# Four transposes of an expert step taken apart and put among the next step's first weight matmuls

## The reference, cut to what matters

```
h = silu(xb @ w_gate[e]) * (xb @ w_up[e])     # 128 rows x inner width
y = h @ w_down[e]                             # 128 rows x 1024
```

## Time and profile before

| | |
|---|---|
| median of 3 runs | 2444.83 us (2444.14 to 2445.98) |
| profiled execution, first to last instruction | 2444.1 us |
| PE busy | 2319.3 us, 95% of the span |
| DVE busy | 1842.5 us, 75% |
| ACT busy | 1472.0 us, 60% |
| instructions | 30601 |
| mean granted TensorE clock | 0.975 |

### The profile page before, as it was taken

The page is one execution under the profiler, slowest core; times in us unless marked ns, Lnnn a source line. Parts: engine busy times, 40 slices in busy tenths (PEclk is TensorE's granted clock), DMA queues, the critical chain, the costliest instruction groups (busy, mean ns, idle before and its releaser), DMA issues.

```text
span 2444.1 us, 30601 instructions
## 1 busy us (share of the span) xinstructions
PE 2319.3 (95%) x12418; PEld 1890.2 (77%) x12418; DVE 1842.5 (75%) x1911; ACT 1472.0 (60%) x1441; POOL 39.0 (2%) x41
## 2 busy tenths in 40 slices
PE   7989989999999998988999998899999999999996
PEld 6778777888888886776788777678888888888885
DVE  5885558888898985676454577588988878888885
ACT  5355437776777774535443653476776767767764
POOL 0100000000000000020000002000000000000000
PEclk8999998999999999999999999899999999999999
DMA  9444446999999996506455451269999989999991
GB/s 233 127 122 143 143 161 218 363 367 359 366 358 366 356 369 213 162 8 192 157 188 181 160 162 53 82 222 363 356 363 361 356 300 346 361 365 357 366 345 40
DMA packets 281225, 617.62 MB, mean 253 GB/s; under 512 B 31848, under 2 KB 130408, under 8 KB 243696
## 3 DMA queue, kind: packets, MB, share of 16 engines
q1 hardware_dynamic: 279664, 611.33, 71.9%
q10 hardware_dynamic: 1408, 4.19, 0.5%
HBM read 612.34 MB, written 1.05 MB: 251 GB/s over the span
## 4 chain that ended last, share of the span: by engine, by line
PE 83%; DVE 10%; ACT 4%; issue 2%; DMA 0%; DVEq 0%; ACTq 0%; SPq 0%
PE ps L566 24%; PE ps L567 24%; PE ps L568 24%; DVE ring_parts L590 3%; ACT high_parts L586 2%; PE ps L2153 1%; PE ps L2809 1%; PE ps L2123 1%; PE ps L3090 1%; PE ps L2124 1%; PE ps L3103 1%; DVE arena L1357 0%; DVE arena L3347 0%; PE ps L1559 0%; PE ps L2164 0%
## 5 line engine op out<-in xcount | busy, mean ns | idle before, releaser
L590 DVE TENSOR_TENSOR ring_parts<-ring,high_parts 128x2048 fp32r<-128x2048 f32 (+1 forms) x574 | 1283.0, 2274 | 172.8 <-ACT high_parts L586 166.8
L586 ACT CAST high_parts<-ring 128x2048 fp32r<-128x2048 f32 (+1 forms) x574 | 1078.7, 1898 | 185.1 <-PE ps L568 181.6
L568 PE MATMUL ps<-high_parts,arena_parts 128*128 128x512 f32 (+2 forms) x1560 | 619.8, 397 | 0.0
L566 PE MATMUL ps<-high_parts,hT_parts 128*128 128x512 f32 (+2 forms) x1120 | 456.9, 408 | 30.4 <-DVE ring_parts L590 12.1
L567 PE MATMUL ps<-ring_parts,hT_parts 128*128 128x512 f32 (+2 forms) x1120 | 445.5, 398 | 0.0
L566 PE MATMUL ps<-high_parts 128*128 128x512 f32 x912 | 365.3, 401 | 0.0
L567 PE MATMUL ps<-ring_parts,high_parts 128*128 128x512 f32 x912 | 359.1, 394 | 0.0
L568 PE MATMUL ps<-high_parts 128*128 128x512 f32 x912 | 356.5, 391 | 0.0
L568 PEld LDWEIGHTS ps<-high_parts,arena_parts 128*128 128x128 f32 x1560 | 299.1, 192 | 68.8
L566 PE MATMUL ps<-high_parts,arena_parts 128*128 128x512 f32 x744 | 293.6, 395 | 5.3 <-DVE arena_parts L1869 2.9
L567 PE MATMUL ps<-ring_parts,arena_parts 128*128 128x512 f32 x744 | 292.7, 393 | 0.0
(11 more groups left out here) (531 smaller groups left out, 1828.0 us busy)
## 6 DMA issues: line engine op xcount, KB each, us to landing
ring<-in_moe_w SPq DMA_DIRECT2D x248, 1024.0 KB, 5.4
ring<-in_w_gate SPq DMA_DIRECT2D x64, 1024.0 KB, 5.3
ring<-in_w_up SPq DMA_DIRECT2D x64, 1024.0 KB, 5.3
ring<-in_w_down SPq DMA_DIRECT2D x64, 1024.0 KB, 5.3
ring<-in_w_in SPq DMA_DIRECT2D x104, 256.0 KB, 4.4
ring<-in_ffn_w SPq DMA_DIRECT2D x44, 512.0 KB, 4.8
ring<-in_w_in SPq DMA_DIRECT2D x20, 1024.0 KB, 5.1
ring<-in_moe_w SPq DMA_DIRECT2D x32, 512.0 KB, 4.9
```

What stands on the lines that cost most here:

```text
L566: pe.matmul(dst, a_hi, b_hi, start=first, stop=False, skip_group_check=True)
L568: return pe.matmul(dst, a_lo, b_hi, start=False, stop=last, skip_group_check=True)
L586: act.copy(high_flat(p), raw_flat(p)).then_inc(upper, 1)
L590: dve.tensor_tensor(raw_flat(p, ring_parts_flat), raw_flat(p), f32(high_flat(p)), ALU.subtract).then_inc(split, 1)
```

## The change

The four transposes of a turn no longer stand together ahead of the next step's first gate piece. A new function `turn_chunk` makes one transpose; `up(st, 0, between)` calls it after each of its four chunks, so that one transpose follows every third matmul. The two waits of `turn` go with the first of the transposes. When the held step is a short one, only the first two chunks are followed by one. At the two kinds of places where a turn is not in front of a plain step (`grouped` steps, the second step of each block, the end of each block) it stays as it was: 75 turns of 80 are moved, 288 transposes of 304. The signal `used` of the piece is still given by its twelfth matmul, in front of the last transpose. The number of instructions that compute something is the same.

```diff
+            def turn_chunk(st, c):
+                nc_ = st.n // P
+                if c == 0:
+                    pe.wait_ge(sig("moe_hid"), st.no)
+                    if st.no > 1:
+                        pe.wait_ge(sig("moe_hidT"), st.no - 1)
+                mm = pe.transpose(ps[:, TURN, c * P:(c + 1) * P], m_hid[:, 0:st.n][:, c::nc_], ident[:])
+                if c == nc_ - 1:
+                    mm.then_inc(sig("moe_turned"), 1)
+
             def turn(st):
-                pe.wait_ge(sig("moe_hid"), st.no)
-                if st.no > 1:
-                    pe.wait_ge(sig("moe_hidT"), st.no - 1)
-                nc_ = st.n // P
-                for c in range(nc_):
-                    mm = pe.transpose(ps[:, TURN, c * P:(c + 1) * P], m_hid[:, 0:st.n][:, c::nc_], ident[:])
-                mm.then_inc(sig("moe_turned"), 1)
+                for c in range(st.n // P):
+                    turn_chunk(st, c)
...
-            def up(st, h):
+            def up(st, h, turned=None):
...
                     mm = matmul3(pe, ps[:, bank, :], hi[:, c, :], lo[:, c, :], a[:, i], b[:, i], c == 0, c == KC - 1)
-                mm.then_inc(used, 1)
+                    if i == 3:
+                        mm.then_inc(used, 1)
+                    if turned and i < turned.n // P:
+                        turn_chunk(turned, i)
...
-                if held and s > 1:
+                grouped = st.first and b % TOGETHER == 0
+                between = held if s > 1 and not grouped else None
+                if s > 1 and grouped:
                     turn(held)
-                grouped = st.first and b % TOGETHER == 0
...
-                up(st, 0)
+                up(st, 0, between)
```

## The result

The changed kernel takes 2466.12 us (median of 6 runs, 2461.41 to 2469.07), the kernel before 2444.48 us (median of 6, 2440.91 to 2448.57). The ratio is 1.0088, 95% interval 1.0076 to 1.0100: slower by 0.9%. Forecast were 2468.4 us in a range of 2460 to 2481. The profiled execution took 2469.07 us; its span is 2467.3 us, 23.2 us over that of the profiled execution of before.

The account below looks back on a forecast made before the run. PE was taken to bound the kernel, busy 95% of the span. Plain steps 0, short steps 18.8 and filled waits 4.8 us gave 23.6 us more: 2468.4 us, range 2460 to 2481.

Parts of the forecast that it names:

- A lone transpose at 0.12 us: On PE, a transpose standing alone costs what one of four does, so plain steps gain or lose nothing.
- the load as described: On PE, the next L566's weight load starts only when the lone transpose starts, which is too short to cover it.
- The short steps at 2.35 us each: In 8 short steps PE's first down L567 comes 2.35 us later because the turned rows come late: 18.8 us.
- the four waits: In a short step: ACT for the turn, DVE for ACT, first down low part for its high part, PE for it.
- The filled waits at 0.48 us each: In 10 steps where the turn stood under PE's wait for DVE, the transposes are now paid in full: 4.8 us.
- Plain steps covered by DVE's idle time: In steps of 512, late rows take 1.14 us of DVE's 2.58 us idle time before `product`, costing nothing.
- The cover of the step behind the short one: DVE's first piece there starts at 10.8 us, its L567 possible at 13.5; PE comes at 14.2, covered by 0.6 us.
- The sum: Plain steps 0, short steps 18.8 and filled waits 4.8 us make 23.6 us on the whole span.
- The clock: Rival: PE's clock falls after the new waits in short steps, 1.6 us lost 8 times, 2481.2 us; 6 in 100.
- ACT's wait for the transposes in the short step: Sign in the profile after: ACT waits near 9.6 us for L2153 in short steps instead of 6.84.
- the first rival: On PE, the weight load behind a lone transpose is hidden, each saving 0.06 us: 2451.3 us; 8 in 100.
- the upper bound of the forecast's own range: An unseen 0.06 us of changeovers between transposes and matmuls for each of 75 turns, given as 2474 us.

Follow-up runs that it names:

- experiment 4: Changed kernel with only 57 of 75 turns apart, in plain steps without a filled wait; against the kernel before ratio 1.0002, block 2 +0.19 us.
- Experiments 1: Changed kernel with only the short steps' turns four in a row again; against the kernel before ratio 1.0012, block 2 +4.50 us.
- 2: Changed kernel with only the turns in front of the 8 short steps apart; against the kernel before ratio 1.0087, block 2 +25.05 us.
- experiment 3: Changed kernel with ACT and DVE making the short steps' down parts ahead of the turned rows' copy; against the kernel before ratio 1.0006.
- 6: All turns four in a row, the short steps' moved behind the step's first chunk; against the kernel before ratio 1.0007, block 2 +2.21 us.
- experiment 7: All turns four in a row, the short steps' moved behind the step's second chunk; against the kernel before ratio 1.0033, block 2 +7.76 us.
- experiment 5: Changed kernel with turns apart only in the 10 steps where PE already waited for DVE's first low part; against the kernel before ratio 1.0015.

## Why the prediction was right

- **The bound** was right: PE sets the pace, and each wait on it came out at the end.
- **A lone transpose at 0.12 us**: 0.34 us to the next L567 where 0.35 was forecast, the load as described, plain steps 17.14 us both ways, and experiment 4 at +0.19 us. The 56 ns of the Trainium skill (TensorE: Matmul & The Clock Gate, Back-to-back issue gap), read as hiding the load behind a lone transpose, would have given 0.29 and a gain; the trace does not agree. The forecast took only half of that section: it gives the 56 ns for an isolated matmul and says itself that this is too little in a stream of weight loads and matmuls, where it has about 81 ns for 128 columns. The 0.11 to 0.12 us measured here is above both.
- **The short steps at 2.35 us each**: 2.36 measured (8.63 less 6.27), with the four waits in the forecast order. Experiments 1 and 2 place them, 3 shows the queue behind the copy to be the cause, 6 and 7 the 0.43 us in hand (6.27 less 5.38 + 0.46).
- **The filled waits at 0.48 us each**: 0.48 on average in experiment 5, from 0.41 to 0.51. The same steps of the changed kernel pay 0.41 to 0.51 as well.
- **Plain steps covered by DVE's idle time**: 1.17 us of it went, where 1.14 was forecast. The cover of the step behind the short one held too: DVE's first piece there starts at 1799.16, 10.7 us after the short step's first matmul (10.8 forecast), and PE doesn't wait for it. No further wait appeared; of PE's 18 waits for L590 in block 2, 8 are the short steps, 9 the filled ones and one was there before.
- **The sum** for block 2 was 18.8 + 9 x 0.48 = 23.1 us. The two executions without a fall of the clock gave 23.3. For block 1 0.48 was forecast, 0.49 measured. The whole program tests the forecast less sharply: its medians differ by 21.6 us where 23.6 was forecast, less than the 23.8 us and more that the traces show in the two stages. The traces don't say where the medians lose these 2 us; the stretch between the stages alone varies by more.
- **The clock** was a rival with 6 in 100 and 8 x 1.6 us. It came true in part, which the forecast had not allowed for: 1 fall of 8 in the profiled execution, +1.5 us. The forecast had set it aside on one stretch in which the clock stayed at 1.00 behind an idle time. That was too little to go by, and that it did little harm was luck: the changed kernel had 1 fall in its 24 such waits in three executions, the two kernels with only the short steps' turns moved had 4 in 8 each time.
- ACT's wait for the transposes in the short step was forecast at 9.6 us and is 8.85. What was left out is the late copy of the plain step in front: behind it ACT is later too, and it ends the short step's two high parts 5.38 us before the step's first PE instruction instead of 6.17. These 0.8 us are missing from its wait. They have no part in the sum, as ACT was waiting in either case.
- Two slips in the sums change nothing: in the first rival 51 x 0.24 is 12.2 and not 12.5, and the upper bound of the forecast's own range comes to 2472.9 and not 2474.

## What to carry to other kernels

When a producer is moved later, look at the whole queue behind its consumer on each engine, not only at the value moved, and look in the shortest stage: the same 2.8 us were free where `down` began 11.6 us into the step and cost 2.35 us where it began 6 us into it. A small instruction in front of a wait is free as long as it fills it; put behind the wait, it is paid in full. Where a consumer waits for a late value at the head of an in-order queue, work that doesn't need the value can go ahead of it, as in experiment 3.

## What the runs showed of the hardware that was not expected

Idle times of PE of the same length, 2.10 to 2.12 us, behind and in front of the same work, were followed by a granted clock of 1.00 in some short steps and by six or seven matmuls at the lower level of 1.2 GHz in others, some 1.5 us more each time. Which ones they were repeated from execution to execution of one kernel (4 of 8, the same four, in 4 executions of two kernels) and changed with moves elsewhere in the stage (0 or 1 of 8 in 3 executions). So an idle time of this length can't be priced by its length alone. Shorter ones in front of this stage's weight matmuls were never followed by a fall: the eight of 0.72 us in experiment 7, and in every version one of 1.1 us and one of 1.5 us.
